# Where the split inputs of each room begin in SBUF, relative to the split weights

## The reference

```
x = x + mix @ w_out[l]
x = x + memory_attention(rms_norm(x, norm_mem_g[l]), ...)
x = x + peer_ffn(rms_norm(x, norm_ffn_g[l]), peer_w_q[l], peer_sub_keys[l], peer_u[l], peer_v[l])
...
h = h + mix                                   # mix: sb_rwkv_mixer, then mla_mixer
h = h + conv_glu(rmsnorm(h, ffn_norm[i]), ffn_w_in[i], ffn_conv_w[i], ffn_conv_b[i], ffn_w_out[i])
h = h + gate * e
```

## Time and profile before

| | |
|---|---|
| time, median of 2 runs | 2019.29 us (2016.72 and 2021.86) |
| the profiled execution, span | 2021.6 us |
| TensorE busy | 1877.1 us (93%), 16,518 matmuls |
| TensorE weight loads busy | 1800.7 us (89%) |
| DVE busy | 1456.5 us (72%) |
| ScalarE busy | 1242.6 us (61%) |
| read from HBM | 293.26 MB, 146 GB/s over the span |

### The profile page before, as it was taken

One profiled execution on the slowest core, in us unless ns is written; L12 is line 12 of the kernel. 1 busy time (PEld: TensorE's weight loads), 2 busy tenths in 40 slices (PEclk: granted clock), 3 DMA queues, 4 the chain that ended last, 5 costly groups with the idle time before them and its releaser, 6 DMA issues. The chain is left out here.

```text
span 2021.6 us, 45016 instructions
## 1 busy us (share of the span) xinstructions
PE 1877.1 (93%) x16518; PEld 1800.7 (89%) x16518; DVE 1456.5 (72%) x3046; ACT 1242.6 (61%) x2420; POOL 0.2 (0%) x4
## 2 busy tenths in 40 slices
PE   8998988999999999999999989687999977999997
PEld 8887888999999976899999989587999976899996
DVE  7667667688985479766666667776888678578857
ACT  5454655777776789655555556733665555666555
POOL 0000000000000000000000000000000000000000
PEclk9999999999999999999999999798999989999998
DMA  6533344466655620266666646101665644166562
GB/s 208 158 97 105 118 143 136 132 194 193 179 186 175 186 84 0 84 194 190 196 191 193 193 139 199 52 3 56 184 196 173 192 126 136 34 190 189 176 198 76
DMA packets 102084, 296.06 MB, mean 146 GB/s; under 512 B 9539, under 2 KB 32454, under 8 KB 101830
## 3 DMA queue, kind: packets, MB, share of 16 engines
q1 hardware_dynamic: 101958, 294.35, 47.0%
HBM read 293.26 MB, written 1.05 MB: 146 GB/s over the span
## 5 line engine op out<-in xcount | busy, mean ns | idle before, releaser
L459 DVE TENSOR_TENSOR w_low<-ring,w_high 128x512 fp32r<-128x512 f32 x1102 | 743.2, 685 | 357.1 <-ACT w_high L453 349.2
L503 PE MATMUL bank<-a_high,w_high 128*128 128x256 f32 x3228 | 921.2, 285 | 74.3 <-DVE w_low L459 39.1
L504 PE MATMUL bank<-a_low,w_high 128*128 128x256 f32 x3228 | 907.5, 281 | 0.0
L505 PE MATMUL bank<-a_high,w_low 128*128 128x256 f32 x3228 | 907.4, 281 | 0.0
L453 ACT ACTIVATE w_high<-ring 128x512 fp32r<-128x512 f32 x1102 | 671.4, 624 | 375.3 <-PE bank L505 372.8
L503 PEld LDWEIGHTS bank<-a_high,w_high 128*128 128x128 f32 x3228 | 620.0, 192 | 90.0 <-DVE w_low L459 39.7
L504 PEld LDWEIGHTS bank<-a_low,w_high 128*128 128x128 f32 x3228 | 616.3, 191 | 0.4
L505 PEld LDWEIGHTS bank<-a_high,w_low 128*128 128x128 f32 x3228 | 616.7, 191 | 0.0
L503 PE MATMUL bank<-s_high,w_high 128*128 128x256 f32 x1024 | 283.5, 277 | 2.0 <-DVE s_low L2446 2.0
L504 PE MATMUL bank<-s_low,w_high 128*128 128x256 f32 x1024 | 283.3, 277 | 0.0
L505 PE MATMUL bank<-s_high,w_low 128*128 128x256 f32 x1024 | 283.3, 277 | 0.0
(11 more groups left out here) (368 smaller groups left out, 1867.8 us busy)
## 6 DMA issues: line engine op xcount, KB each, us to landing
ring<-in_stream SPq DMA_DIRECT2D x273, 512.0 KB, 3.7
ring<-in_peer_u SPq DMA_DIRECT2D x128, 512.0 KB, 3.6
ring<-in_peer_v SPq DMA_DIRECT2D x128, 512.0 KB, 3.5
ring<-in_stream SPq DMA_DIRECT2D x32, 256.0 KB, 3.3
ring<-in_stream SPq DMA_DIRECT2D x12, 192.0 KB, 2.7
x<-in_x SPq DMA_DIRECT2D x4, 256.0 KB, 6.3
arena<-in_mem SPq DMA_DIRECT2D x1, 1024.0 KB, 11.0
out<-x SPq DMA_DIRECT2D x4, 256.0 KB, 2.6
```

What stands on the lines that cost most here:

```text
L459: self.nc.vector.tensor_tensor(self.cut(h, self.w_low), self.raw(h), self.cut(h, self.w_high.bitcast(F32)), ALU.subtract)\
L503: self.nc.tensor.matmul(to, lh, rh, start=start, stop=False, **more)
L504: self.nc.tensor.matmul(to, lh, rl, start=False, stop=False, **more)
L505: return self.nc.tensor.matmul(to, ll, rh, start=False, stop=stop, **more)
```

## The change

The arenas get a few floats more at their end (`lift`), which moves the split inputs behind them, and in the PEER room a tensor of 16 floats that nothing uses (`s_lift`) stands ahead of s_high. HYBRID_ROOM shrinks by 256 floats, two times 512 bytes, which makes space and leaves the distance modulo 512 alone. An arena begins where it did, and everything that is placed in it, but for a scratch area at the end of the hybrid room's, which moves down by 1,024 bytes.

```diff
-HYBRID_ROOM = 31488
+HYBRID_ROOM = 31232
...
-    def room(self, floats, chunks=0):
-
+    def room(self, floats, chunks=0, lift=0):
...
-        with self.nc.sbuf_tensor(f"arena{self.rooms}", [P, floats], F32) as self.arena:
+        with self.nc.sbuf_tensor(f"arena{self.rooms}", [P, floats + lift], F32) as self.arena:
...
-        with self.room(N_KEYS * T):
+        with self.room(N_KEYS * T, 0, 32):
...
-            with self.nc.sbuf_tensor("s_high", [P, SIDES, T], F32R) as s_high, \
+            with self.nc.sbuf_tensor("s_lift", [P, 16], F32), \
+                    self.nc.sbuf_tensor("s_high", [P, SIDES, T], F32R) as s_high, \
...
-        with k.room(86 * T, 2 * DC):
+        with k.room(86 * T, 2 * DC, 16):
...
-        with k.room(HYBRID_ROOM, DC + 3):
+        with k.room(HYBRID_ROOM, DC + 3, 64):
...
-        with k.room(70 * T, DC + FC + 2):
+        with k.room(70 * T, DC + FC + 2, 96):
```

## The result

The changed kernel took 2060.66 us (median of two runs, 2057.08 and 2064.24) against 2019.29 before: 1.0199 times as long, with a 95% interval of 1.0141 to 1.0257. It is slower, by about 41 us; whether by more than 2% these two runs leave open. Two of the other executions of the kernel before took 2677.86 and 4710.44 us, far from all the rest, and are left out of what follows. The changed kernel's profiled execution has a span of 2062.5 us, 40.9 more than the one of before.

A forecast was written before the change was run, and what follows sets the result against it. The prediction took TensorE's matmul pace to bound the kernel. To 2019.3 us it added 4 us for more slow matmuls and nothing for the rest: 2023 us, range 1990 to 2078.

The forecast's parts named there:

- within 2%: Whole kernel: time changes by no more than 2%; chance 0.67, likeliest 2023 us, own range 2000 to 2058.
- the slower rival: 256-wide matmuls: inputs passing the weight load mid-load cost 16 ns, 122.7 each, giving about 2110 us; chance 0.24.
- What bounds the kernel: Whole kernel: TensorE, busy 93% of the span, bounds it; what matmuls cost is what the kernel costs.
- Cost of nothing for the rest: Matmuls from hot or arena, ScalarE and DVE: no cost; 512-wide matmuls could move by at most 2.7 us.
- the step that read the earlier trace as a sign of the passing: 512-wide matmuls, inputs 64 bytes ahead: 229.3 ns against 213.3, 16 ns over, taken to support that distance matters.
- the two known paces are only drawn anew: All split matmuls: bursts still run at 113.3 or 117.9 ns, changing the time by -19 to +38 us.
- a share of slow matmuls of 40%: All 12,756 matmuls: the slow share goes from 34% to 40%, adding 4 us.
- this term of the sum: Added cost of more slow matmuls: 0.07 x 12,756 x 4.5 ns = +4 us.
- The bound of +38 us: All split matmuls: the cost if every burst fell slow, (12,756 - 4,300) x 4.5 ns.
- the one pass that was wholly fast could only lose: Second expert pass: 3,054 matmuls, wholly fast before, can lose 14 us at the slow pace.
- Its decision point: Slower rival: decides from 40 us, 3.1 ns on the mean matmul, 118.0 ns.
- The rival without effect: Split matmuls: distance does not matter, the load's phase sets the pace; 2019 us within 5; chance 0.22.

## Why the prediction was right and wrong

The time, 2060.7, fell into the range (1990 to 2078), and within 2% had the most chance. But it lies 38 us above the likeliest value and 3 above the end of that case's own range (2058). That it fell inside is in part luck: the range had been stretched upward for the slower rival, whose mechanism failed too, and 1.0199 is on the very edge of "within".

**What bounds the kernel: right.** About 38 of the 41 us came from the pace of matmuls, with the same counts, the same clock in the six stretches, and the other engines waiting longer; the other 3 are the clock outside those stretches.

**Cost of nothing for the rest: right.** The float32 matmuls from the arena, DVE and ScalarE did not move. Nor did the 512-wide matmuls at the distances of the change, for which I had left 2.7 us. In the kernel with distance 256 (TensorE's timeline, 15 matmuls between):

```profile
1301.32 0.39 PE L503 MATMUL bank<-w_high,a_high 128*128 128x512 f32 x1
...
1304.72 0.39 PE L503 MATMUL bank<-w_high,a_high 128*128 128x512 f32 x1
```

That is 3.40 us for 15, 226.7 ns, against 229.3 in the earlier trace rows; their mean is 229 to 230 at 448, 192, 0 and 256 alike. This also takes the support from the step that read the earlier trace rows as a sign of the passing. They are not blind to the distance, though: at 384, 416 and 480 their mean is 233.

**Failed: "the two known paces are only drawn anew", with "a share of slow matmuls of 40%".** I took the two paces as fixed by the hardware and only their shares as open, and so priced a room at a new distance between 113.3 and 117.8. The distance decides which paces exist at all. At 448 and 192 there are 113.3 and 117.8; at 64 and 320 it is 117.8 with 3% and 6% of the matmuls at 113.3; at 128 it is 118.7; at 0 it is 120.0. Nor are the shares drawn: many bursts fall the same way in every profile. The mean from start to start, over all rooms, is 117.9 in the changed kernel and was 114.9: 12,756 x 3.0 = 38 us, where this term of the sum had 4. The bound of +38 us was nearly the result because it stands for "the fast pace is gone everywhere", and that is what happened outside the hybrid room. That the one pass that was wholly fast could only lose was right; it lost 16 us of the 41, more than the 14 that 117.8 would cost. Two small slips in the sum change nothing of this: from 34% to 40% are 0.06 and 3 us, not 0.07 and 4, and the last room could lose 9 us by its own count of slow matmuls, not 7.

**Failed: the mechanism of the slower rival.** A passing of two addresses once per 512 bytes would be dearest in the middle of a load and cheapest at distance 0. Measured, 0 is the dearest with 256, half a period away in that picture, and 192, which passes at 5/8, is as good as 448. Its decision point, 118.0 ns on the mean, was nearly met all the same, with paces of 117.5 to 119.5 in four rooms and none at 122.7.

**The rival without effect fell**: 448 everywhere and 0 everywhere differ by 2.2%, in the same order of instructions. The Trainium skill, SBUF — State Buffer, section "Who interferes with whom", says PE never waits on anyone; by that the distance was worth 0, and these runs show TensorE at 113.3 or 120.0 ns by where its operands lie. That its two reads hold each other up would explain it, but no run shows the wait itself.

**Also missed: the spread of the kernel before.** I had read in the earlier trace rows that a short break flips the pace, but did not draw from it that whole executions must differ by a second pass that is fast or slow. Two runs 5 us apart hid that; more showed 23 us.

## What to carry to other kernels

Where TensorE streams one block of weights after another at full clock, read its pace from start to start, stage by stage, and compare it over stages and executions: here one instruction had 113.3, 117.8 and 120.0 ns, and nothing on the page but a mean length shows it. Look at every stage before a distance is called good or bad: at 416 and 464 one pass alone gave the wrong picture. Then the place of the moving tensor relative to the weights is a tuning knob, worth 2% in this kernel, and one that any added or removed tensor ahead of them turns by accident; it should be asserted in the code once a good distance is known. A kernel with two paces also needs more than two runs before a change of 1% can be judged.

## What the runs showed of the hardware

- The pace of float32r matmuls (256 columns, a new 128 x 128 block each) depends on the distance from moving to loaded operand with a period of 256 bytes: 120.0 ns at 0 and 256, 117.8 at 64 and 320 (with a few at 113.3), 118.7 at 128 and 384, 113.3 or 117.8 at 192 and 448. Between them, 416 gave 117.3 or 118.7, 432 119.3, 464 116.7 or 119.2, and 480 118.3. That the period is 256 rests on three pairs: 0 and 256, 128 and 384, 192 and 448 (64 and 320 agree too, each in one room).
- It depends on the distance and not on the addresses: moved together by 64 bytes, or inputs by 512, nothing changed (ratios 1.0001 and 1.0006). The distance from w_high is not the whole of it: with that at 448 and all behind w_high moved by 192 bytes, the paces were 117.8 and 122.2.
- At one distance two patterns can be stable, at 448 and 192 each for hundreds of microseconds, with none or one of three weight loads 4 ns longer. Many bursts take the same one in every profile, others do not.
- At half clock the same matmuls took 213.3 ns at distance 448, their columns and nothing else, and they take as long at 0, where the effect is largest at full clock. In the kernel of distance 0, head of the hybrid room, 22 matmuls in 4.48 us (20 between these):

```profile
1226.63 0.42 PE L504 MATMUL bank<-a_low,w_high 128*128 128x256 f32 x1
...
1231.11 0.31 PE L504 MATMUL bank<-a_low,w_high 128*128 128x256 f32 x1
```

- Which access holds up which is not known, nor why 192 modulo 256 is the good one.
